# Modulation weights loaded as two contraction chunks by 2048 columns, one column strip of TensorE for each quarter of the columns

## The reference

```
def modulation(cvec, lw):
    m = jax.nn.silu(cvec) @ lw["ada_w"] + lw["ada_b"]
    return jnp.split(m[..., None, :], 6, axis=-1)

sh1, sc1, g1, sh2, sc2, g2 = modulation(c, lw)
h = modulate(rms_norm(x, lw["norm1_g"]), sh1, sc1)
zq, zk, zv, zqkv, zg, zb, za = jnp.split(h @ lw["w_in"], SPLITS, axis=-1)
...                                  # attention and gated delta rule side by side
x = x + g1 * (o_mix @ lw["w_out"])
x = x + g2 * hier_moe(modulate(rms_norm(x, lw["norm2_g"]), sh2, sc2), lw)
```

## Time and profile before

| | us |
|---|---|
| median of 3 runs | 1374.74 |
| lowest, highest | 1372.54, 1381.22 |
| the profiled execution | 1372.78 |
| its span in the profile | 1371.0 |

### The profile page before, as it was taken

How to read it: one execution, slowest core, us unless ns; L and a number is a source line. 1 busy time by engine, 2 the same in 40 slices (tenths; PEclk the granted TensorE clock), 3 DMA queues, 4 the chain that set the end, 5 groups by cost and what they waited for, 6 DMA issues and landing times.

```text
span 1371.0 us, 21250 instructions
## 1 busy us (share of the span) xinstructions
PE 1256.0 (92%) x8943; PEld 616.6 (45%) x8943; DVE 577.2 (42%) x1478; ACT 310.4 (23%) x743; POOL 91.3 (7%) x104
## 2 busy tenths in 40 slices
PE   4999996899978999999989999969899699999996
PEld 1565544575553333333346554537556333333332
DVE  1266977464353212121262687945625412121215
ACT  0237412223131010101022661223322210101010
POOL 0020011110010000000021000021000100000001
PEclk9899998899988999999999999979999899999998
DMA  9550144868765999999675012275595589999994
GB/s 339 187 151 0 62 149 115 269 229 307 295 241 185 339 399 396 400 397 399 271 291 161 0 62 85 83 199 200 185 347 174 199 289 392 397 397 399 395 397 162
DMA packets 172690, 340.86 MB, mean 249 GB/s; under 512 B 34463, under 2 KB 36903, under 8 KB 172583
## 3 DMA queue, kind: packets, MB, share of 16 engines
q1 hardware_dynamic: 164807, 312.82, 63.5%
q0 software_dynamic: 7776, 26.55, 5.3%
HBM read 318.64 MB, written 20.71 MB: 248 GB/s over the span
## 4 chain that ended last, share of the span: by engine, by line
PE 71%; DVE 13%; DMA 9%; SPq 4%; issue 2%; ACT 1%; POOL 0%; POOLq 0%; DVEq 0%; ACTq 0%
PE bank L513 67%; PE bank L516 4%; DVE ring L1671 3%; DMA ring<-in_moe_w_dram 3%; DVE arena L1671 2%; DMA ring<-in_ada_w_dram 1%; DMA ring<-in_w_in_dram 1%; DVE arena L1679 1%; DVE small L1679 1%; DMA arena<-tok_dram,idx 1%; SPq L1255 1%; DMA raw_dram<-ring 1%; SPq L1202 1%; SPq L1213 1%; DVE x L1679 1%
## 5 line engine op out<-in xcount | busy, mean ns | idle before, releaser
L513 PE MATMUL bank<-ring,arena 128*32 128x512 f32 (+1 forms) x3088 | 469.6, 588 | 4.8 <-ACT arena L1363 2.9
L513 PE MATMUL bank<-arena 128*32 128x512 f32 (+4 forms) x2160 | 377.9, 530 | 28.8 <-DVE arena L1671 21.6
L1363 ACT ACTIVATE arena<-bank 128x512 f32<-128x512 f32 (+3 forms) x320 | 143.1, 479 | 612.6 <-PE bank L516 328.8
L513 PE MATMUL bank<-ring,hT 128*128 128x512 f32 x576 | 254.5, 597 | 2.4 <-DMA ring<-in_w_in_dram 2.4
L513 PEld LDWEIGHTS bank<-ring,arena 128*32 128x32 f32 (+1 forms) x3088 | 139.6, 114 | 223.0 <-issue 223.0
L513 PEld LDWEIGHTS bank<-arena 128*32 128x32 f32 (+3 forms) x2160 | 130.8, 127 | 162.8 <-issue 124.0
L513 PEld LDWEIGHTS bank<-ring,hT 128*128 128x128 f32 x576 | 108.2, 192 | 128.6 <-issue 125.8
L1671 DVE TENSOR_TENSOR hT<-hT,bank 128x512 f32<-128x512 f32 x24 | 16.5, 687 | 335.0 <-PE bank L513 335.0
L513 PE MATMUL bank<-hT,ring 128*128 128x384 f32 x384 | 132.3, 501 | 0.0
L513 PEld LDWEIGHTS bank<-hT,ring 128*128 128x128 f32 x384 | 73.7, 196 | 48.4 <-issue 4.2
L516 PE MATMUL bank<-const,arena 128*128 128x128 f32 x347 | 52.0, 288 | 33.4 <-DMA arena<-tok_dram,idx 19.6
(11 more groups left out here) (139 smaller groups left out, 905.7 us busy)
## 6 DMA issues: line engine op xcount, KB each, us to landing
ring<-in_moe_w_dram SPq DMA_DIRECT2D x62, 2048.0 KB, 16.7
arena<-in_moe_w_dram SPq DMA_DIRECT2D x34, 2048.0 KB, 18.6
ring<-in_ada_w_dram SPq DMA_DIRECT2D x24, 2048.0 KB, 8.9
ring<-in_w_in_dram SPq DMA_DIRECT2D x14, 2048.0 KB, 9.7
expert_dram<-arena SPq DMA_DIRECT2D x22, 512.0 KB, 15.9
ring<-in_w_out_dram SPq DMA_DIRECT2D x4, 2048.0 KB, 8.5
arena<-in_na_rpb_dram SPq DMA_DIRECT2D x32, 96.0 KB, 4.7
tok_dram<-arena POOLq DMA_DIRECT2D x6, 512.0 KB, 4.0
```

The costliest lines, as they stand in the source:

```text
L513: return nc.tensor.matmul(out, lhsT, rhs, start=start, stop=stop)
L1363: return nc.scalar.activation(out, in_, func, **kw)
```

## The change

An ada slab now holds two contraction chunks for 2048 columns, in pieces of 2048 numbers: slab j of a layer is chunk pair j % 4 of column group j // 4. It has the same bytes as before, in 256 pieces of 8 KB. Its slot is read as [chunk, quarter, 512]. For each of its two chunks, strip q of TensorE multiplies quarter q of the columns, with the same stationary columns in all four strips; the sum over all eight chunks is made in the bank, over four slabs. `silu_w` needs no padding (256 columns in place of 304), and the table "pick" selects one row of each strip where it summed four. The number, shape and order of the instructions on each engine are the same as before.

```
-    parts["pick"] = (t[:, None] % 32) == np.arange(2 * SHARE)[None, :]
+    parts["pick"] = t[:, None] == (np.arange(2 * SHARE) // 2 * 32 + np.arange(2 * SHARE) % 2)[None, :]
...
-        silu_w = sb("silu_w", [P, KC, 32 + 2 * (SHARE - 1)])
+        silu_w = sb("silu_w", [P, KC, 32])
...
-                w = wide(pre_slot[slab])
-                first = 2 * (SHARE - 1 - at)
-                for k in range(KC):
-                    q = k % 4
-                    last = mm(bank[3][32 * q:32 * q + 32, :], silu_w[:, k, first:first + 32], w[:, k, :],
-                              at == 0 and k < 4, at == SHARE - 1 and k >= 4)
+                w = slot(pre_slot[slab]).rearrange("p (k q n) -> p k q n", k=2, q=4)
+                for i in range(2):
+                    k = 2 * at + i
+                    for q in range(4):
+                        last = mm(bank[3][32 * q:32 * q + 32, :], silu_w[:, k, :], w[:, i, q, :], k == 0, k == KC - 1)
...
-                    src = weights[layer].rearrange("(k p) n -> p k n", p=P)[:, :, j * 512:(j + 1) * 512]
-                    sp.dma_start(wide(pre_slot[name]), src).then_inc(slab_in[pre_slot[name]], 16)
+                    src, dst = weights[layer].rearrange("(k p) n -> p k n", p=P), wide(pre_slot[name])
+                    if kind == "ada":
+                        group, at = divmod(j, SHARE)
+                        src = src[:, 2 * at:2 * at + 2, 2048 * group:2048 * (group + 1)]
+                        dst = slot(pre_slot[name]).rearrange("p (k n) -> p k n", k=2)
+                    else:
+                        src = src[:, :, j * 512:(j + 1) * 512]
+                    sp.dma_start(dst, src).then_inc(slab_in[pre_slot[name]], 16)
...
-            tt(silu_w[:, :, 2 * SHARE - 2:2 * SHARE], silu_c[:].rearrange("p (s k) -> p k s", s=2),
+            tt(silu_w[:, :, 0:2], silu_c[:].rearrange("p (s k) -> p k s", s=2),
```

## The result

| | before | after |
|---|---|---|
| median of 20 runs | 1375.95 us | 1372.47 us |
| lowest, highest | 1372.54, 1383.65 | 1367.78, 1375.90 |
| profiled execution (span) | 1372.78 (1371.0) | 1370.53 (1368.7) |

The ratio of after to before is 0.9965, with a 95% interval of 0.9953 to 0.9977: 4.8 us less, 3.2 to 6.5 by the interval, and 3.5 by the two medians. Beside other kernels on a later chip the same kernel gave 0.9976 (0.9961 to 0.9991), 3.3 us, 1.2 to 5.4 by the interval. The forecast was 3.1 us less and 1371.6.

What follows compares the result with a forecast made beforehand. TensorE, busy 92% of the span, was taken to carry most of the chain, with loads binding only in places; 1.76 + 3 x 0.44 = 3.08, say 3.1 us, off 1374.74 gave 1371.6, range 1366.6 to 1376.4.

Steps and rivals of the forecast that it cites:

- The rate: Ada loads: 8 KB packets would run at 420 GB/s, a slab falling from 5.43 to 4.99 us, 0.44 less.
- the rival with this rule: Ada loads: line rate from 512 B on, so 2 KB pieces leave nothing to gain; 1374.7 us, within a rival of chance 0.22.
- The rest of the edit: TensorE products, pick table and smaller memset: no cost, no gain; sixteen records still 1.92 us at full clock.
- The start, -1.76: Kernel start: four ada slabs ahead of w_in's first, each 0.44 us shorter, bring the path forward 1.76 us, and this is kept.
- The price of a packet: DMA engines, all loads: each packet costs 9.2 ns once plus 75.7 ns for each 2 KB.
- The inverses' write, -0.44: At 229.23, write of the inverses to DRAM: begins when the ada load ahead of it has drained, 0.44 us sooner.
- The load behind the short rows, -0.44: At 245.85, ada load behind eight short-row loads: drains 0.44 us faster; with the write's gain, TensorE's wait shrinks from 1.23 to 0.35.
- The load at 317.66, -0.44: Mixing stage, an ada load of its own: 0.44 us shorter out of a 2.73 us wait of TensorE.
- The clock's further gain: Around the two mixing-stage waits: shorter waits keep TensorE at 2.4 GHz, another 3.95 us gone, 1367.6; chance 0.15.
- No change: Whole kernel: the rate does not rise, or a later stage gives the gain back; 1374.7 us; chance 0.22.
- slow large packets: Ada loads: 8 KB pieces run at 224 GB/s like instruction fetches, a slab 3.93 us more, 1402 in all; chance 0.05.
- The expert stage as a place that gives the gain back: Expert stage: if bound by a transfer starting at a fixed time, an earlier start is worth nothing; 1374.7, within chance 0.22.

Runs made afterwards that it cites:

- e1_2kb: Changed kernel with ada loads cut back to 2 KB pieces, two transfers per slab; ratio to before 1.0003 (0.9987 to 1.0018).
- e12_change_again: The changed kernel as it is, run and profiled again beside other kernels on a later chip; ratio to before 0.9976 (0.9961 to 0.9991).
- e10_start_512b: Changed kernel, two transfers per slab, 512 B pieces in the first four ada slabs, 8 KB in the other twenty; ratio to before 1.0035.
- e4_start_8kb: Changed kernel, two transfers per slab, 8 KB pieces only in the first four ada slabs, 2 KB in the other twenty; ratio to before 0.9985.
- e9_mixing_512b: Changed kernel, two transfers per slab, 8 KB pieces in the first four ada slabs, 512 B in the other twenty; ratio to before 1.0039.
- e6_experts_16kb: Changed kernel, with expert weights also read in 16 KB pieces and tokens transposed to match; ratio to before 0.9968 (0.9947 to 0.9989).
- e5_mixing_8kb: Changed kernel, two transfers per slab, 2 KB pieces in the first four ada slabs, 8 KB in the other twenty; ratio to before 1.0006.
- e11_experts_and_latents: Changed kernel plus expert slabs in 16 KB pieces and the latents loaded behind the first w_in slab; ratio to before 0.9979 (0.9965 to 0.9993).

## Why the prediction was right, point by point

*The rate.* Right. 420 GB/s was worked out for 8 KB from the rates of 2 and 4 KB; 421 was measured. Other profiles with 8 KB pieces there gave 417 to 421. The same two numbers gave 291 for 512 B, and 293 was measured. The Trainium skill, DMA: Bandwidth & Descriptors (Specifications), would have line rate from 512 B on and about 358 GB/s as one core's share of HBM. The traces disagree with the first (293 GB/s at 512 B, 387 at 2 KB, 421 at 8 KB), and the rival with this rule falls. They go past the second; no run here has a second core at work, so whether it holds as a share is not shown.

*The rest of the edit.* Right: free within 2 us, by e1_2kb.

*The start, -1.76.* Right in place, and a little small: 1.91 in after and 2.12 in e12_change_again (36.85). The price of a packet gives 4 x (5.43 - 4.98) = 1.8 with the measured 421 GB/s; the rest may lie in how the loads begin and was not followed up. That a loss there is kept to the end is shown by e10_start_512b; that the gain is kept, by the point of e4_start_8kb (2.1 us) and not by its interval.

*The inverses' write, -0.44.* Too large. From its issue to the reading back it took 6.38 us before and 6.13 in e12_change_again, 0.25 less; with 512 B pieces ahead of it (e9_mixing_512b) 6.14, with 2 KB pieces (e4_start_8kb) 6.08. So the size of the pieces ahead hardly sets it, and the step "begins when the ada load ahead of it has drained: -0.44" failed. The slab's head start may matter more. In after it was issued 6.19 us ahead of the write, not 4.68 as in before, and the way took 5.37 us; in e1_2kb, with 2 KB pieces and 5.54 us, 5.66. But in e6_experts_16kb it took 6.11 with a head start of 5.18, so this stays a reading.

*The load behind the short rows, -0.44.* Too large. The chain's row is 12.47 us before. In e12_change_again this is the row of the chain, and then that of the timeline for its product:

```profile
242.98 12.38 DMA ring<-in_ada_w_dram
```

```profile
255.41 3.64 PE L513 MATMUL bank<-ring,silu_w 128*32 128x512 f32 x16 [1.11 <-DMA ring<-in_ada_w_dram]
```

0.09 less, and the wait of TensorE is 1.11 and not 0.35. In after the wait is gone: the slab was issued later, at 247.13, behind a product that ran slow until 247.06, and yet was there by 257.93. The other kernels say the same of the size. From the issue to the product it took 12.52 us in before, 12.26 with 2 KB pieces in e4_start_8kb, 12.43 and 12.47 with 8 KB in e12_change_again and e5_mixing_8kb, and 13.31 with 512 B in e9_mixing_512b. Its beginning is slow whatever the pieces. In e12_change_again the DMA engines moved 140 GB/s from 242 to 245 us and 196 from 245 to 249, while the last of the short rows had not landed, and 413 from 249 to 253; in before 132 from 245 to 248, 201 from 248 to 252 and then 397. So about half of its time goes by at under half the rate. That the short rows are the cause is likely and not shown; no kernel took them away.

*The load at 317.66, -0.44.* Too large, and for another reason. The load is 7.80 us before and 7.69 in e12_change_again, 7.44 in e11_experts_and_latents, but the step that failed is the one behind it: "What is late next there is the product at 332.04, which now runs without a wait". VectorE's chain was late next, within 0.1 us in before. This place paid 0.06 in after and nothing in e12_change_again; against e4_start_8kb and e1_2kb, where TensorE ran slow for longer behind that product, it would be 0.3 and 1.3.

So of the forecast sum of 3.08 the traces bear out 1.8 to 2.1 at the start, and of the 1.32 in the mixing stage at most some 0.3 to 0.4. Even that is below what single executions scatter by. From the first issue of the inverses' write to the twelfth late product before took 104.12 us, e12_change_again 103.61 and e4_start_8kb, with 2 KB pieces there, 103.18, but after 101.58. What the ratios have above 2.1 to 2.5 (3.3 and 4.8 us) lies within the interval in the one case and beyond it in the other. It is not located: the end of the first layer's expert products is 3.1 us earlier in e12_change_again and 3.8 in after,

```profile
659.98 20.78 PE bank L513 x192
```

```profile
659.27 20.74 PE bank L513 x192
```

against 663.10 before (rows of the chain, e12_change_again first), and differences of the granted clock between single executions are as large (0.958 before, 0.961 after, 0.955 in e12_change_again over the whole). That the forecast of 3.1 came out so near 3.3 is therefore in part luck: its three terms of the mixing stage were together about 1 us too large, and something that no trace locates made up for it. The prediction's text also speaks of five transfers where it lists and counts four; the sum has the four.

*The rivals.* The clock's further gain: in after the two products took 2.83 and 2.39 us, not 3.64 and 3.43, in e12_change_again 3.64 and 3.55. So it comes and goes from one execution to the next, and behind the second place of before it would have been worth 0.1 us. No change, slow large packets: excluded. The expert stage as a place that gives the gain back: excluded by e6_experts_16kb and e10_start_512b.

## What to carry to other kernels

Fit the price of a packet from two piece sizes in the kernel's own trace and draw it out; here it gave two other sizes within 1%. Then count only the places where the chain runs through such a load, and at each ask two things. What else shares the engines with the load: behind the short rows it ran at half rate and its piece size did not show. And what stands right behind the wait: at the start nothing did, and the first product moved by all of the gain; at the last place of the mixing stage another engine's chain stood 0.1 us behind, so faster loads were worth almost nothing there while slower ones cost. A small share that cannot be measured can be settled by making the same cause five times larger, but only in the direction in which it is made larger. And run the same kernel twice before reading a late row of one trace: two executions here parted by 2.7 us in a stretch without any load that the change touches.

## What the runs showed of the hardware beyond that

Four ada loads kept SyncE for 12.52 us when each had 1024 pieces and for 2.13 us with 256; with it the latents' load is issued at 6.34 and not 16.72 us. The bytes were the same, so the queue's room goes by pieces and not by bytes, as far as these two show. SyncE is not freed by it: in after it is held next in the two w_in loads (21.07 us from 6.86 on), whose 1024 pieces each are unchanged. Pieces of 8 KB were single packets (663 packets for 4.63 MB, of which 155 smaller).
